# Sums of squares of the second mixer's keys and of the third mixer's latents, as two products on a rounded part and a rest

## The reference, cut to what matters

```python
def rms_norm(x, gain):
    xf = x.astype(jnp.float32)
    y = xf * lax.rsqrt(jnp.mean(xf * xf, axis=-1, keepdims=True) + EPS)
    return (y * gain.astype(jnp.float32)).astype(x.dtype)

k, v = jnp.split(rms_norm(h, kv_norm) @ w_kv, 2, axis=-1)
k = rms_norm(k.reshape(b_, s_, SB_HEADS, SB_DH), k_gain)      # 8 heads of 128
```

```python
q = rms_norm_2(q_lat, q_a_norm_g) @ w_q_b       # q_lat: 256 wide
kv = rms_norm_2(c_kv, kv_a_norm_g) @ w_kv_b     # c_kv: 128 wide
```

## Time and profile before

| | |
|---|---|
| median of the runs | 2237.23 us |
| the profiled execution | 2236.99 us |
| its span in the trace | 2234.9 us |
| PE busy | 2207.3 us, 99% of the span |
| DVE busy | 1104.0 us, 49% |
| ACT busy | 927.2 us, 41% |
| POOL busy | 291.5 us, 13% |
| granted TensorE clock, mean | 0.999 |

### The profile page before, as it was taken

How to read it: one execution, slowest core, us unless ns; L and a number is a source line. 1 busy time by engine, 2 the same in 40 slices (tenths; PEclk the granted TensorE clock), 3 DMA queues, 4 the chain that set the end, 5 groups by cost and what they waited for, 6 DMA issues and landing times.

```text
span 2234.9 us, 28526 instructions
## 1 busy us (share of the span) xinstructions
PE 2207.3 (99%) x11122; PEld 1809.6 (81%) x11122; DVE 1104.0 (49%) x1411; ACT 927.2 (41%) x1255; POOL 291.5 (13%) x247
## 2 busy tenths in 40 slices
PE   9999999999999999999999999999999999999998
PEld 6888888788888888877888888888778778888887
DVE  6655656454443233554444433355666565555522
ACT  5445554242222234564432222245565564444312
POOL 0211112310000110003100001100000034222211
PEclk9999999999999999999999999999999999999999
DMA  3311111122222222201222222421221223222221
GB/s 137 113 57 38 57 38 39 58 96 102 102 94 94 94 94 76 95 20 57 95 94 94 94 96 97 146 95 57 72 70 40 72 82 108 94 96 103 102 95 57
DMA packets 31773, 185.39 MB, mean 83 GB/s; under 512 B 3120, under 2 KB 7728, under 8 KB 11328
## 3 DMA queue, kind: packets, MB, share of 16 engines
q1 hardware_dynamic: 29664, 176.46, 22.5%
q0 software_dynamic: 2016, 7.60, 1.0%
HBM read 179.83 MB, written 7.37 MB: 84 GB/s over the span
## 4 chain that ended last, share of the span: by engine, by line
PE 94%; DVE 2%; ACT 2%; issue 1%; DMA 0%; POOL 0%; DVEq 0%; SPq 0%; POOLq 0%; ACTq 0%
PE ps L1807 26%; PE ps L1809 25%; PE ps L1808 25%; PE ps L2050 2%; PE ps L2535 1%; PE ps L2044 1%; PE ps L2478 1%; PE ps L2518 1%; PE ps L2313 1%; PE ps L2545 1%; PE ps L2353 1%; PE ps L2071 1%; PE ps L2476 0%; PE ps L2128 0%; PE ps L2001 0%
## 5 line engine op out<-in xcount | busy, mean ns | idle before, releaser
L1807 PE MATMUL ps<-xh,wh 128*128 128x512 f32 x1888 | 764.0, 405 | 2.9 <-POOL xl L1757 2.1
L1809 PE MATMUL ps<-xh,wl 128*128 128x512 f32 x1888 | 736.9, 390 | 0.0
L1808 PE MATMUL ps<-xl,wh 128*128 128x512 f32 x1888 | 735.9, 390 | 0.0
L360 ACT ACTIVATE wh<-raw 128x2048 fp32r<-128x2048 f32 x143 | 273.8, 1914 | 540.3 <-PE ps L1809 540.0
L964 DVE TENSOR_TENSOR wl<-raw,wh 128x2048 fp32r<-128x2048 f32 x143 | 330.0, 2307 | 313.4 <-ACT wh L360 313.4
L1807 PEld LDWEIGHTS ps<-xh,wh 128*128 128x128 f32 x1888 | 355.1, 188 | 82.2 <-issue 14.6
L1809 PEld LDWEIGHTS ps<-xh,wl 128*128 128x128 f32 x1888 | 354.4, 188 | 76.1
L1808 PEld LDWEIGHTS ps<-xl,wh 128*128 128x128 f32 x1888 | 355.3, 188 | 70.4 <-issue 4.8
L1807 PE MATMUL ps<-hid_h,wh 128*128 128x512 f32 (+1 forms) x550 | 211.9, 385 | 0.0
L1809 PE MATMUL ps<-hid_h,wl 128*128 128x512 f32 (+1 forms) x550 | 210.6, 383 | 0.0
L1808 PE MATMUL ps<-hid_l,wh 128*128 128x512 f32 (+1 forms) x550 | 208.7, 379 | 0.0
(11 more groups left out here) (365 smaller groups left out, 2835.4 us busy)
## 6 DMA issues: line engine op xcount, KB each, us to landing
raw<-in_stream SPq DMA_DIRECT2D x159, 1024.0 KB, 4.8
hankd<-tabd SPq DMA_DIRECT2D x1, 3072.0 KB, 17.2
hank<-hankd POOLq DMA_DIRECT2D x4, 768.0 KB, 5.0
hT<-in_xT SPq DMA_DIRECT2D x4, 512.0 KB, 6.7
keepd<-hT POOLq DMA_DIRECT2D x1, 2048.0 KB, 10.2
hT<-keepd POOLq DMA_DIRECT2D x8, 256.0 KB, 4.4
out<-hT SPq DMA_DIRECT2D x8, 256.0 KB, 2.6
raw<-in_stream SPq DMA_DIRECT2D x2, 512.0 KB, 8.9
```

Source lines behind the costliest of these rows:

```text
L360: act.activation(wh[:, s, :], raw[:, s, :], ACT.Copy).then_inc(hi_made, 1)
L1807: pe.matmul(out, w_hi, a_hi, start=start, stop=False)
L1808: pe.matmul(out, w_hi, a_lo, start=False, stop=False)
L1809: return pe.matmul(out, w_lo, a_hi, start=False, stop=stop)
```

## The change

Squares are now rounded to fp32r by ACT, DVE makes the rest, and PE sums both parts with two products in fp32r in place of one in the full type.

For the keys, `k_evac` gets a second ACT instruction after the square (it waits for the square's own counter), `k_low` on DVE follows `k_in`, and `k_squares` has four products in place of two. The two parts lie in the buffers `soft_h` and `soft_l`, which a later phase uses. The ones come from `exact`, so the first `k_squares` waits for `exact_made`.

For the latents, ACT makes an fp32r copy of the ones and of each square, DVE makes the rests behind its second evacuation, and PE has six products in place of three. The parts lie in `qws` and `qrs`, which are free then.

```diff
         def k_evac(i):
             act.activation(q_sb[:, :, :], qk_raw[:, :, :], ACT.Square).then_inc(k_sq, 1)
+            act.wait_ge(k_sq, i + 1)
+            act.activation(k_sq_h, q_sb[:, :, :], ACT.Copy).then_inc(k_sq_hi, 1)
...
+        def k_low(i):
+            dve.wait_ge(k_sq_hi, AGAIN + i + 1)
+            if i:
+                dve.wait_ge(k_ss, i)
+            dve.tensor_tensor(k_sq_l, q_sb[:, :, :], k_sq_h.bitcast(F32), ALU.subtract).then_inc(k_sq_lo, 1)
...
             k_in(i)
+            k_low(i)
...
         def k_squares(i):
-            pe.wait_ge(k_sq, i + 1)
+            pe.wait_ge(k_sq_hi, AGAIN + i + 1)
+            pe.wait_ge(k_sq_lo, AGAIN + i + 1)
             if i:
                 pe.wait_ge(k_ln, i)
-            pe.matmul(ps[:, 4, :], mat("ones"), q_sb[:, 0, :], start=True, stop=True)
-            pe.matmul(ps[:, 5, :], mat("ones"), q_sb[:, 1, :], start=True, stop=True).then_inc(k_ss, 1)
+            else:
+                pe.wait_ge(exact_made, START_IN + 4)
+            for a in range(2):
+                pe.matmul(ps[:, 4 + a, :], ones_r, k_sq_h[:, a, :], start=True, stop=False)
+                m = pe.matmul(ps[:, 4 + a, :], ones_r, k_sq_l[:, a, :], start=False, stop=True)
+            m.then_inc(k_ss, 1)
...
                 act.activation(dst, src, ACT.Square).then_inc(lat_sq, 1)
+                act.wait_ge(lat_sq, i + 1)
+                if i == 0:
+                    act.activation(lat_ones[:, :], mat("ones"), ACT.Copy)
+                    act.activation(qws[:, 0, :, :], qn[:, :, :], ACT.Copy).then_inc(lat_sq_hi, 1)
+                else:
+                    act.activation(qws[:, 1, 0, :], kn[:, 0, :], ACT.Copy).then_inc(lat_sq_hi, 1)
...
+            if i == 1:
+                dve.wait_ge(lat_sq_hi, AGAIN + 1)
+                dve.tensor_tensor(qrs[:, :, :], qn[:, :, :], qws[:, 0, :, :].bitcast(F32), ALU.subtract).then_inc(lat_sq_lo, 1)
+                dve.wait_ge(lat_sq_hi, AGAIN + 2)
+                dve.tensor_tensor(qws[:, 1, 1, :], kn[:, 0, :], qws[:, 1, 0, :].bitcast(F32), ALU.subtract).then_inc(lat_sq_lo, 1)
...
                 if i == 2 and j == 8:
-                    pe.wait_ge(lat_sq, 2)
-                    pe.matmul(ps[:, 4, :], mat("ones"), qn[:, 0, :], start=True, stop=False)
-                    pe.matmul(ps[:, 4, :], mat("ones"), qn[:, 1, :], start=False, stop=True).then_inc(lat_ss, 1)
-                    pe.matmul(ps[:, 5, :], mat("ones"), kn[:, 0, :], start=True, stop=True).then_inc(lat_ss, 1)
+                    pe.wait_ge(lat_sq_hi, AGAIN + 2)
+                    pe.wait_ge(lat_sq_lo, AGAIN + 2)
+                    for c in range(3):
+                        pe.matmul(ps[:, 4 + c // 2, :], lat_ones[:, :], lat_sq_h[c], start=c != 1, stop=False)
+                        m = pe.matmul(ps[:, 4 + c // 2, :], lat_ones[:, :], lat_sq_l[c], start=False, stop=c != 0)
+                        if c:
+                            m.then_inc(lat_ss, 1)
```

More of the change, by code:

```diff
@@ L205, in build @@
             ident_r, future_r, suffix_r, ones_r = [exact[:, k, :] for k in range(4)]
+            k_sq_h, k_sq_l = [t[:, 0:2 * SEQ].rearrange("p (a n) -> p a n", a=2) for t in (soft_h, soft_l)]
         with ExitStack() as mix:
@@ L218, in build @@
             qws = sb("qws", [P, 2, 2, SEQ], F32R, mix)
+            lat_ones = sb("lat_ones", [P, P], F32R, mix)
+            lat_sq_h, lat_sq_l = [qws[:, 0, a, :] for a in range(2)] + [qws[:, 1, 0, :]], [qrs[:, a, :] for a in range(2)] + [qws[:, 1, 1, :]]
             prob = sb("prob", [P, 3, 768], F32, mix)
@@ L299, in build @@
          half_filled, latent_done, kr_hi, kr_lo, kb_hi, nsink_made, pv_done, tr_done, pt_act, pt_dve,
-         sc_done, qw_lo, kb_val, rcol_done, rcol_made) = (
+         sc_done, qw_lo, kb_val, rcol_done, rcol_made, k_sq_hi, k_sq_lo, lat_sq_hi, lat_sq_lo) = (
             ss_done, rqk_ln, rqk_made, qkn_made, picked, rows_done, eg_made, e_min, dt_made,
             tb_made, kk_done, attn_qk_done, at_made, attn_made, qd_made, kt_done, vt_done, kdkbe_made, vb_made,
-            amt_done, w_done, w_made, o_sq, oss_done)
+            amt_done, w_done, w_made, o_sq, oss_done, qk_silu, qk_sq, o_ln, o_rstd)
         block = ctx.enter_context(nc.Block())
```

## The result

The changed kernel takes 2245.02 us (median of 7 runs, 2244.35 to 2245.47) against 2237.23 us: a ratio of 1.0035, with a 95% interval of 1.0026 to 1.0044. It is slower by 7.8 us, where 5.6 were forecast, and lies 0.2 us over the end of the range. Of all the runs in this document one stands apart: a run of the kernel with the sums 4 blocks later took 2243.99 us at a mean granted clock of 0.948, where its ten neighbours had 0.998 or 0.999; it has no profile, and no median hangs on it.

A forecast was written before the change was run, and what follows sets the result against it. PE, busy for 99% of the span, was taken as the bound. Keys +6.35 us (3 x 1.62 + 1.49) and latents -0.76 us sum to +5.59 us, so the median 2237.23 becomes 2242.8 us; range 2241.4 to 2244.8.

The forecast's parts named there:

- The chain between square and sum: Keys, between square and sum: ACT's rounding and DVE's subtraction take 2.40 us, with 0.11 us between the engines.
- PE's start at the first sums: First key sums: ready at 830.15, so PE starts them 2.34 us later than at 827.81.
- That nothing of it is hidden: Key sums: all of the delay is stall, since PE takes its list in order; 2.34 us at the first.
- The savings on PE: Key and latent sums: fp32r products save 0.82 us unstalled at a key sum, 0.81 at the last; latents 1.21.
- The new stall at unit 4 of the latents: Latents, first product of unit 4: PE waits 0.35 us for the split, ready at 1482.15 when PE comes at 1481.80.
- The splits costed at nothing: Keys' phase, later splits on ACT and DVE: covered by slack, cost nothing; uncovered, at most 1 to 3 us each.
- the first rival: Behind the four key stalls the clock falls, 2.1 us more each, +8.4, or 2251.2 us; chance 0.04.
- The sign that was named for this: PE's products behind the key stalls: steps of 0.4 us or more there would show the prediction wrong.
- the second rival: More waits than counted, above all a late split behind longer ACT and DVE lists: 2244.8 to 2247 us; chance 0.07.

The follow-up runs named there:

- the kernel with the sums 4 blocks later: Whole change with the key sums 4 blocks later in PE's list, against the kernel before: 2232.05 us, ratio 0.9976; again 2232.89 us, ratio 0.9983.
- the kernel with the latents only: The change to the latents alone, keys summed in the full type as before, against the kernel before: 2235.97 us, ratio 0.9993.

## Why the prediction was wrong

**Right, to a tenth of a us or so.** The chain between square and sum: 2.40 us for rounding and rest, read from another place of the trace, were 827.83 to 830.15 here, 2.32, since DVE starts 0.03 us behind ACT and not 0.11; PE starts 0.10 us behind DVE and not 0.05. PE's start at the first sums was forecast at 830.15 and came at 830.12. That nothing of it is hidden, since PE keeps its order: shown by the four waits. The savings on PE, 4.03 us unstalled, are what the kernel with later sums has (4.1 by the marks). The new stall at unit 4 of the latents, 0.35 us forecast, 0.38 measured, and gone when the split was moved. The splits costed at nothing cost nothing: PE has no wait on them in the keys' phase.

**Wrong: the clock.** The forecast's sum has no term for a clock that falls behind the stalls; it was put at nothing, and measured 3.19 us. The step that failed is in the first rival: "after the 1.77 us idle PE goes on with steps of 0.31 and 0.23 us, the full pace". One idle of 1.77 us without a fall was taken as evidence that idles of 2.2 us are harmless, and the rival got a chance of 0.04. The profile of before had only that one idle near the length in question, and the forecast put four beyond it. The runs show that at 2.0 to 2.2 us a fall is about as likely as not: 7 behind 14 such stalls. The idle of 1.77 us was read rightly, it has no fall in any profile; what failed is the step from it to 2.2 us. The sign that was named for this, steps of 0.4 us or more behind the stalls, is what the profile shows (0.43). The price was mis-sized as well: 2.1 us for a fall, from the start of the kernel, against 1.6 us; and all four stalls were counted, where two had one. A middle case, two falls in four at 1.6 to 2.1 us, would have been 2246 to 2247 us, and the range should have reached to it. The time itself, 2245.0, lies where the second rival stood (2244.8 to 2247, by a split that is late), but no split was late.

That the forecast missed by so little is in part luck. The changed kernel's marks are 8.65 us, 3.1 over the sum of 5.59; the 0.75 us less at the end of the kernel, which nobody had counted, took a quarter of that back.

The Trainium skill ("TensorE: Matmul & The Clock Gate", Part 1) has PE's clock go down to half when it stands idle for long enough. With the halving the traces agree: 0.50 granted behind the stalls. The prediction says that the page leaves open how an idle of 2.2 us stands to it; by the page's rule 2.2 us is too short as well. There the measurement decides: falls behind 7 of 14 idles of 2.0 to 2.2 us.

**The medians.** 7.8 us of the medians stand against 8.65 of the marks less 0.75 of the end. In the same way the other medians lie within 0.4 us of their marks less the end, but for the first job of the kernel with the sums 4 blocks later (0.7), and the two kernels whose own runs lie over 4 us apart (0.7 and 1.0). The medians of the kernel before in the four jobs lie between 2237.04 and 2237.6, so the tenths of this comparison carry nothing.

What stays open: what decides whether an idle of given length is followed by a fall. Of three idles of 3.5 us one had none, of fourteen of 2.0 to 2.2 us seven had one. Nor does a fall begin at a fixed distance from the idle: it begins within two of the 3.5 us idles, and 1 us behind the end of the changed kernel's first. No run here tells why.

## What to carry to other kernels

Where PE is the bound and its inputs come just in time, work put between the last step and PE costs its full length, and may cost half a clock on top: count an idle of 2 us as some 3 us. Before a cheaper product is paid for with longer preparation, look how far the consumer can be moved back in PE's list; here 4 blocks turned +7.8 us into -4.5 to -5.5 (by the marks, +8.65 into -4.1). And a gain on PE moves the next late producer into view: 0.4 of the latents' 1.2 us were lost at a split that had been 0.8 us early.

## What the runs showed of the hardware that was not expected

The clock can fall to half behind 2.0 to 2.2 us of idle (7 of 14) and stay up behind 3.5 us (1 of 3). It stays down for some 3.4 us, most of it work, and once, behind the third stall of the kernel with its sums 2 blocks earlier, for nearly 7 (0.50 from 862.8 to 869.5).

At the start of the kernel PE works at half pace although the windows give a granted clock of 1.00. That 1.00, which the first rival of the prediction quotes, is not a measurement: the clock's record in the trace begins only at 8.6 us in the profile before, and at 10.8 us in that of the kernel with the latents only, and a stretch without a record counts as 1.00. The products reach their full pace where the record begins. The moment differs from run to run: a sum in the full type that began at 10.15 us in the profile before begins at 11.28 in that of the kernel with the latents only, whose list is the same up to there.

```profile
4.67 2.93 PE L1969 MATMUL ps<-mats 128*128 128x128 f32 x12 [4.67 <-DMA mats<-in_mats]
7.39 1.91 PE L1975 MATMUL ps<-om_gdn,mats 128*128 128x512 f32 x2
9.10 2.34 PE L1969 MATMUL ps<-mats 128*128 128x128 f32 x12
11.28 1.02 PE L1975 MATMUL ps<-om_gdn,mats 128*128 128x512 f32 x2
```

Against the earlier trace rows that is 1.1 us which no change has made. Where one kernel has two profiles, such a difference makes up 0.46 of 0.62 us of span (the changed kernel) and 1.04 of 1.06 (the sums 4 blocks later), as the norm of the keys' phase shows. So it is most of what separates these runs, and the reason why two marks inside the trace tell more than the medians where less than 1 us is at stake.
